# Three output tiles abreast in the first feed-forward of the second network

## What is computed

```python
def dwconv3(x, w, b):
    xp = jnp.pad(x, ((0, 0), (1, 1), (0, 0)))
    return xp[:, :-2] * w[0] + xp[:, 1:-1] * w[1] + xp[:, 2:] * w[2] + b

def conv_ffn(h, w_in, conv_w, conv_b, w_out):
    a = dwconv3(h @ w_in, conv_w, conv_b)
    gate, up = jnp.split(a, 2, axis=-1)
    return (jax.nn.silu(gate) * up) @ w_out
```

## Time and profile before

| | us |
|---|---|
| median of three runs | 2185.72 |
| lowest and highest | 2183.20, 2185.84 |
| span of the profiled execution | 2184.7 |
| TensorE busy in it | 2080.9 (95%) |
| DVE busy | 1622.3 (74%) |
| ACT busy | 1153.5 (53%) |

### The profile page before, as it was taken

One profiled execution on the slowest core, in us unless ns is written; L12 is line 12 of the kernel. 1 busy time (PEld: TensorE's weight loads), 2 busy tenths in 40 slices (PEclk: granted clock), 3 DMA queues, 4 the chain that ended last, 5 costly groups with the idle time before them and its releaser, 6 DMA issues.

```text
span 2184.7 us, 36761 instructions
## 1 busy us (share of the span) xinstructions
PE 2080.9 (95%) x13916; PEld 1867.6 (85%) x13916; DVE 1622.3 (74%) x2677; ACT 1153.5 (53%) x2045; POOL 106.6 (5%) x186
## 2 busy tenths in 40 slices
PE   4999999999999999999998899999998999999998
PEld 3988989999988989998866587887877888999998
DVE  7688878955778879946877788687778526757984
ACT  4547756645556756645635455252534235656762
POOL 2100000000100000000000000001000000000000
PEclk9999999999999999999999999999999999999999
DMA  7766556854766547855441433546553222244553
GB/s 296 283 232 205 178 174 223 268 190 164 276 226 202 174 156 258 282 173 178 140 146 49 144 116 136 183 144 205 187 177 116 97 92 100 89 144 132 188 178 114
DMA packets 106895, 383.02 MB, mean 175 GB/s; under 512 B 11632, under 2 KB 16368, under 8 KB 105456
## 3 DMA queue, kind: packets, MB, share of 16 engines
q1 hardware_dynamic: 78304, 282.23, 38.3%
q0 software_dynamic: 25344, 92.29, 12.4%
q10 hardware_dynamic: 3088, 6.29, 0.8%
HBM read 379.71 MB, written 1.05 MB: 174 GB/s over the span
## 4 chain that ended last, share of the span: by engine, by line
PE 85%; DVE 9%; ACT 3%; DMA 2%; issue 2%; DVEq 0%; SPq 0%; ACTq 0%
PE ps L984 22%; PE ps L988 21%; PE ps L987 21%; PE ps L1003 3%; PE ps L1006 3%; PE ps L1007 3%; DVE ada_junk L2088 3%; PE ps L1023 1%; PE ps L1440 1%; DVE ring_l L2063 1%; PE ps L1026 1%; PE ps L1027 1%; ACT ring_r L1490 1%; PE ps L1217 1%; DMA ring<-tape_in 1%
## 5 line engine op out<-in xcount | busy, mean ns | idle before, releaser
L984 PE MATMUL ps<-part,ring_l 128*128 128x256 f32 (+1 forms) x3536 | 1084.9, 307 | 20.3 <-DVE part L2063 16.5
L988 PE MATMUL ps<-part,ring_r 128*128 128x256 f32 (+1 forms) x3536 | 1074.5, 304 | 0.0
L987 PE MATMUL ps<-part,ring_r 128*128 128x256 f32 (+1 forms) x3536 | 1073.4, 304 | 0.0
L1490 ACT ACTIVATE ring_r<-ring 128x1024 fp32r<-128x1024 f32 x511 | 530.8, 1056 | 438.9 <-DMA ring<-tape_in 318.2
L2063 DVE TENSOR_TENSOR ring_l<-ring,ring_r 128x1024 fp32r<-128x1024 f32 x511 | 617.6, 1220 | 168.9 <-ACT ring_r L1490 166.4
L984 PEld LDWEIGHTS ps<-part,ring_l 128*128 128x128 f32 x3536 | 666.9, 189 | 60.7 <-DVE part L2063 21.5
L988 PEld LDWEIGHTS ps<-part,ring_r 128*128 128x128 f32 x3536 | 665.2, 188 | 30.9
L987 PEld LDWEIGHTS ps<-part,ring_r 128*128 128x128 f32 x3536 | 666.9, 189 | 29.0
L2088 DVE SCALAR_TENSOR_TENSOR ada_junk<-work 128x1024 bf16<-128x1024 f32 x272 | 337.7, 1242 | 47.7 <-DMA work<-adas_in 35.1
L1003 PE MATMUL ps<-ring_l,part 128*128 128x512 f32 x264 | 104.7, 396 | 0.2 <-DVE part L2508 0.2
L1006 PE MATMUL ps<-ring_r,part 128*128 128x512 f32 x264 | 104.3, 395 | 0.0
(11 more groups left out here) (247 smaller groups left out, 2039.8 us busy)
## 6 DMA issues: line engine op xcount, KB each, us to landing
ring<-tape_in SPq DMA_DIRECT2D x514, 512.0 KB, 3.4
work<-adas_in POOLq DMA_DIRECT2D x176, 512.0 KB, 4.6
work<-ada_first_in SPq DMA_DIRECT2D x8, 1024.0 KB, 13.3
work<-bias_in ACTq DMA_DIRECT2D x1, 2048.0 KB, 8.1
x<-x_t_in SPq DMA_DIRECT2D x1, 1024.0 KB, 15.8
work<-cond_in SPq DMA_DIRECT2D x1, 1024.0 KB, 18.2
x<-ctx_in ACTq DMA_DIRECT2D x1, 1024.0 KB, 15.7
x<-dist_in ACTq DMA_DIRECT2D x1, 1024.0 KB, 6.9
```

What stands on the lines that cost most here:

```text
L984: mm = pe.matmul(dst, lhsT=wl, rhs=mr, start=(k == 0), stop=False)
L987: pe.matmul(dst, lhsT=wr, rhs=mr, start=False, stop=False)
L988: mm = pe.matmul(dst, lhsT=wr, rhs=ml, start=False, stop=(k == len(moving) - 1))
L1490: act.activation(ring_r[:, q % RING, :], ring[:, q % RING, :], ACT.Copy).then_inc(rounded, 1)
```

## The change

In the first feed-forward of the second network the first three output tiles of each part are computed abreast: at every hidden tile there are three matmuls for each of the three, and then the next hidden tile. The other five follow one by one as before. In the second feed-forward the number is one. The tape is laid out in the new order.

```diff
+OUT_ABREAST = (3, 1)
...
     for c, (first, last) in enumerate(parts_of(j)):
         halves = [w[n * KD:(n + 1) * KD] for f in made_before(j, c) for n in (f, FT + f)]
         out += [abreast(*halves[:ABREAST])] + halves[ABREAST:] if c == 0 else halves
-        out += [stationary(w_out[first * P:last * P])]
+        half = stationary(w_out[first * P:last * P])
+        n_k = last - first
+        out += [abreast(*(half[f * n_k:(f + 1) * n_k] for f in range(OUT_ABREAST[j]))), half[OUT_ABREAST[j] * n_k:]]
     return panels(out)
...
                     for name in names:
                         project2(name, uk)
-                    for f in range(KD):
-                        project2(f"out{1 + 2 * j}_{c}_{f}", [(h_r[:, k % slots, :], h_l[:, k % slots, :]) for k in range(first, last)],
-                                 (lambda k: hidden2_made(j * FT + first + k)) if f == 0 else None)
+                    outs = [f"out{1 + 2 * j}_{c}_{f}" for f in range(KD)]
+                    hk = [(h_r[:, k % slots, :], h_l[:, k % slots, :]) for k in range(first, last)]
+                    project2_abreast(outs[:OUT_ABREAST[j]], hk, lambda k: hidden2_made(j * FT + first + k))
+                    for name in outs[OUT_ABREAST[j]:]:
+                        project2(name, hk)
                 stat_summed(1 + 2 * j, n)
```

## The result

| | before | after |
|---|---|---|
| median, us | 2185.78 | 2167.97 |
| lowest and highest of four runs | 2183.2 to 2186.8 | 2167.0 to 2171.2 |
| span of the profiled execution | 2184.7 | 2165.6 |

The ratio is 0.9912 (95% interval 0.9893 to 0.9931): 17.8 us less, where the prediction gave 18.7 less (2167.1). Two later series of the same kernel gave 2169.25 (ratio 0.9922, 0.9903 to 0.9941) and 2171.35 (0.9938, 0.9921 to 0.9955).

A forecast was written before the change was run, and what follows sets the result against it. TensorE, 85% of the chain, was taken to lose 18.35 us waiting for late hidden tiles and at slowed clock. Span 2184.7 less 18.35, plus 1.0 to the median, less half of 0.6, gave 2167.1 us; range 2163.5 to 2172.

The forecast's parts named there:

- Sum of what is lost: At the three parts' output starts, waits and slow clock cost TensorE 4.57, 5.27 and 8.51 us, together 18.35.
- All seven waits go; margins: At the three output starts every hidden tile is ready before TensorE asks, by 2.0 to 6.7 us; gain 18.35.
- The rival on part 3: Part of the waits comes back in part 3, costing 1 to 4 us, about 2170; chance 0.07.
- Pace and banks: In the output tiles abreast, matmuls follow at 0.229 us and switching banks costs nil.
- The pace term: Behind part 3's start, matmuls at 0.2334 us might return to 0.229, saving 0.6 us; half put in.
- The rival of a slow pace over the whole stage: All the stage's matmuls take 0.2334 us instead of 0.229, costing 6.4 us, 2173.5; chance 0.05.
- the bunched eviction: Three output tiles ending together in each part expose their adds, costing 6.1 us, 2173.2; chance 0.02.
- DVE in part 2, panels: In part 2 DVE's later adds cost 0, at most 1.8 us; panel splits keep a 5.4 us margin, cost 0.
- The lag into part 3's conv groups: DVE enters part 3's conv groups 3.8 us late and meets 2.83 us of idle time; cost 0, at most 1.8.
- Part 3's end: DVE, some 4 us behind at tile 3, catches up by tile 7; cost 0, at most 1 us.
- The total: For the whole kernel, the median of 2185.72 us falls to 2167.4, or 2167.1 with half the pace saving.

The follow-up runs named there:

- clock_filled: The unchanged kernel with matmuls on constants, sized to the waits, put ahead of the last hidden tiles' waits; 2182.9 us, ratio 0.9986.
- two_abreast: The changed kernel with two output tiles abreast in each part instead of three; 2168.36 us, ratio 0.9914.
- products_later: The unchanged kernel with the conditioning products of each part's last conv pair moved behind its last hidden tile; 2184.6 us, ratio 0.9987.
- after_b: The changed kernel run again without any edit; 2164.0 to 2174.5 us in six runs.
- second_too: The changed kernel with two output tiles abreast in the second feed-forward too; 2166.17 us, and 2166.44 when repeated.
- part3_only: The unchanged kernel with three output tiles abreast in part 3 alone; 2179.27 us, ratio 0.9964.
- six_abreast: The changed kernel with six output tiles abreast in each part instead of three; 2201.79 us, ratio 1.0065.

## Why the prediction was right, point by point

- **Sum of what is lost.** Predicted 4.57, 5.27 and 8.51, together 18.35; the starts gave 4.58, 5.28 and 8.66. The split into 12.72 of waits and 5.63 of slow clock is borne out by clock_filled: 13.06 and 5.46. The Trainium skill (TensorE: Matmul & The Clock Gate, Terms) would have made 6.7 of the slow time; the measured 5.46 is nearer to the sum from rows. By place the rule gives 1.76, 1.62 and 3.36 against 1.58, 1.61 and 2.27: the difference lies in part 3, where the clock was already at 0.50 during the last wait (1601.85 to 1603.29).
- **All seven waits go; margins.** Predicted 6.7; 5.7 and 4.7; 3.6, 2.6 and 2.0. In after, DVE's last hidden tile of part 3,

```profile
1595.53 0.69 DVE L2068 TENSOR_TENSOR part<-work,part 128x512 fp32r<-128x512 f32 x1 [0.70 <-ACT part L1832]
```

  is there at 1596.2, and TensorE asks for it at 1585.71 + 54 x 0.229 = 1598.1: a margin of 1.9. The others, worked out likewise, are 6.8; 5.8 and 4.7; 3.7 and 2.5. The rival on part 3 is what two_abreast shows.
- **Pace and banks.** 0.2289 with three banks in turn, no wait to open one. The pace term, 0.6 and put in at half, came whole: 0.47 behind start 3 and 0.15 of its 8.66. That was luck: the prediction tied it to the fall of the clock, and products_later had the fall without the slower pace. The rival of a slow pace over the whole stage didn't come. Nor did the bunched eviction: the three adds lie closer together than before, and yet the stage is 1580 intervals of 0.2289. The Trainium skill (Perfetto Trace Analysis, Matmuls) wants groups to rotate through banks so that one's eviction lies beside the next group's matmuls. Three that end together cost nothing here; with four and six the bunched adds do cost, through what DVE does behind them (the splits, and the norm at the stage's end).
- **DVE in part 2, panels.** Tile 0 was let go at 13.2 us behind the part's start (13.5 predicted). The two splits end at 1508.3, and TensorE gets to the first of the panels at 1481.34 + 33.0 = 1514.3: 6.0, predicted 5.4. Four abreast puts the first split 7.9 us later behind the part's start (32.5 against 24.6), and that margin is gone; hence the 0.63.
- **The lag into part 3's conv groups.** 3.8 us predicted, of which 2.8 meet idle time. In after:

```profile
1529.41 0.74 DVE L2556 SCALAR_TENSOR_TENSOR work<-ps,par,work 128x510 f32<-128x510 f32 x1
...
1532.24 0.75 DVE L2556 SCALAR_TENSOR_TENSOR work<-ps,par,work 128x510 f32<-128x510 f32 x1 [0.17 <-ACT work L1814]
```

  The first tap starts without idle time before it, some 3 us behind its turn (its wait of 1.45 in the earlier trace rows is gone); the next conv group's waits for ACT again. The lag is absorbed within one group, but for some 0.4 us.
- **Part 3's end.** The adds of output tiles 3, 6 and 7:

```profile
1608.59 0.68 DVE L2609 TENSOR_TENSOR work<-work,ps 128x512 f32<-128x512 f32 x1
...
1619.56 0.69 DVE L2609 TENSOR_TENSOR work<-work,ps 128x512 f32<-128x512 f32 x1 [0.44 <-PE ps L991]
...
1624.37 0.69 DVE L2609 TENSOR_TENSOR work<-work,ps 128x512 f32<-128x512 f32 x1 [1.24 <-PE ps L991]
```

  Tile 3 is 3.3 us behind TensorE (4 predicted), and from tile 6 on DVE waits for TensorE again. Four abreast shows what this term is when DVE doesn't catch up: 2.8 us. ACT rounds the last panel 3.2 us behind TensorE's end (3.0 predicted), as in the earlier trace rows:

```profile
1627.53 1.06 ACT L1495 ACTIVATE ring_r<-ring 128x1024 fp32r<-128x1024 f32 x1 [1.75 <-DMA ring<-tape_in]
```

- **The total.** 2167.1 against 2167.97, and 18.65 us of gain against 18.99 in the stage. The gain is understood; that the median fits so closely is in part luck, since the same kernel's three medians spread over 3.4 us while its three traces have the same stage. The prediction's plus or minus 3.4 (2163.5 to 2170.5) holds two of the three medians, the stated top of 2172 the third, 2171.35, and neither holds all single runs. The 1.0 us between span and median compared two different executions; where both are known of one, its time is 2.2 us above its span (2167.76 and 2165.6). The sum is thus the median less the gain.

## What to carry to other kernels

Where a stage's first sum runs into tiles that are still being made, the work that needs only the early ones can be put in front of the wait; two sums abreast got 16.4 of the 19.0 us here, three all, four lost some of it again, and six turned it into a loss, because what is ordered behind the finished sums (here the splits of the next weights) moves back with them. Compute three margins for each number abreast: when the late tile is asked for, when the next weights are, and how far behind the engine that empties the banks is when the stage ends. Cutting DVE's own work in front of a late tile gave little, since the chain ran over ACT.

## What the runs showed of the hardware

**Two paces at full clock.** The same matmuls follow one another at one of two paces, both at a granted clock of 1.00 and without idle time. The second feed-forward (256 columns) in after, and in after_b, the same kernel:

```profile
1972.00:2092.00 120.00, 120.00 (x1021) 120.00 (x1021) 106.16 (x184) 90.42 (x163) 0.00 (x0) 1.00 0.57 188
```

```profile
1972.00:2092.00 120.00, 120.00 (x1061) 120.00 (x1060) 110.48 (x190) 94.77 (x173) 0.00 (x0) 1.00 0.59 195
```

1021 matmuls against 1061 in 120 us; from start to start they are 0.1178 and 0.1133 us. With 512 columns the two are 0.2334 and 0.2289: the slower pace is 0.0045 us more a matmul at either width. It can change from one execution to the next and within one (in after it is the faster one from 2103 us on). Over this stretch it is worth some 4.5 us, more than the 3.4 by which the medians differ; how much of their spread it makes up wasn't measured. What sets it was not found.

**The same idle time, with and without a fall of the clock.** In front of the second feed-forward's first conv group TensorE waits 2.68 us in all thirteen traces. In ten of them the clock falls there, in three (second_too, part3_only, six_abreast) it doesn't. The table of stretches for the 5 us from about that wait's end on, after first and second_too below:

```profile
1904.00:1909.00 5.00, 4.76 (x27) 4.79 (x28) 3.82 (x10) 2.04 (x4) 0.00 (x0) 0.66 0.00 0
```

```profile
1903.00:1908.00 5.00, 4.76 (x39) 4.74 (x40) 3.81 (x10) 2.04 (x4) 0.00 (x0) 1.00 0.13 28
```

27 matmuls in one and 39 in the other. At the starts of before, waits of 2.1 us and less, two or three of them, were each time followed by a fall; two waits of 0.99 and 1.86 us in products_later and of 0.98 and 1.06 us in two_abreast were not. So the 1.6 to 2.3 us of slow clock behind such waits are a price that an execution may or may not pay. Where the wait was taken away, or all but filled with other matmuls, no trace has a fall at these starts.
